# Reordering the products of a blocked down projection so that a norm can lie inside it

## The reference

```python
    gate, up = jnp.split(hn @ w_gate_up, 2, axis=-1)
    return h + (jax.nn.silu(gate) * up) @ w_down          # D_FF = 2816
...
    x = rms_norm(h, final_g)[:, N_META:]                  # end of the first block
...
    h = rms_norm_2(x, pre_norm_g[layer])                  # start of the second block
    proj = h @ w_in[layer]
    a_u, a_v, sq, sk, sv, mq, z = jnp.split(proj, split_at, axis=-1)
    mkv = rms_norm_2(mem, mem_norm_g[layer]) @ w_mem_kv[layer]     # 256 memory rows
```

## Time and profile before

| | |
|---|---|
| Time, 3 runs | 2336.96, 2339.67, 2341.39 us; median 2339.67 |
| The profiled execution | 2337.65 us, of it span 2335.9 us from first to last instruction |
| PE busy | 2195.0 us, 94% of the span |
| DVE, ACT, POOL busy | 1434.1, 907.7, 1013.5 us |
| Granted TensorE clock, mean | 0.976 of 2.4 GHz |
| Down projection on PE | from 1589.8 us to 1805.5 us of the span |
| First turn of x on PE | at 1872.86 us |

### The profile page before, as it was taken

The page is one execution under the profiler, slowest core; times in us unless marked ns, Lnnn a source line. Parts: engine busy times, 40 slices in busy tenths (PEclk is TensorE's granted clock), DMA queues, the critical chain, the costliest instruction groups (busy, mean ns, idle before and its releaser), DMA issues.

```text
span 2335.9 us, 29848 instructions
## 1 busy us (share of the span) xinstructions
PE 2195.0 (94%) x10756; PEld 1807.1 (77%) x10756; DVE 1434.1 (61%) x2790; ACT 907.7 (39%) x1626; POOL 1013.5 (43%) x584
## 2 busy tenths in 40 slices
PE   7999999999999989999989999999999798998896
PEld 6886688998887767778768888888887676878774
DVE  4258799999903567653886565655477607207713
ACT  5234522233225655433433233334445334126622
POOL 1265333465553232236665555555588413120042
PEclk9999999999999989999999999999999799999998
DMA  5112111111242221056244544457754121110212
GB/s 183 52 46 68 55 55 45 55 46 41 73 125 87 64 95 41 28 171 194 86 140 140 171 140 172 140 191 276 250 187 138 44 101 39 52 55 6 91 42 89
DMA packets 244837, 237.94 MB, mean 102 GB/s; under 512 B 10449, under 2 KB 186222, under 8 KB 244702
## 3 DMA queue, kind: packets, MB, share of 16 engines
q1 hardware_dynamic: 240544, 222.97, 29.3%
q10 hardware_dynamic: 4158, 13.16, 1.4%
HBM read 174.01 MB, written 61.15 MB: 101 GB/s over the span
## 4 chain that ended last, share of the span: by engine, by line
PE 71%; DVE 10%; ACT 3%; issue 3%; POOL 1%; DMA 0%; ACTq 0%; DVEq 0%; SPq 0%
PE ps L927 23%; PE ps L1214 16%; PE ps L1239 9%; PE ps L1283 8%; PE ps L1104 6%; PE ps L1438 4%; PE ps L1136 1%; DVE logit L2213 1%; PE ps L1079 1%; PE ps L1122 1%; ACT p_s L2035 1%; DVE pt_lo L2232 1%; PE ps L1361 0%; DVE logit L2226 0%; DVE yz L2757 0%
## 5 line engine op out<-in xcount | busy, mean ns | idle before, releaser
L2810 POOL TENSOR_TENSOR w_lo<-w_raw,w_hi 128x1024 fp32r<-128x1024 f32 (+1 forms) x143 | 312.5, 2186 | 877.3 <-ACT w_hi L1470 877.3
L927 PE MATMUL ps<-x_hi,w_hi 128*128 128x512 f32 (+2 forms) x960 | 361.6, 377 | 4.0 <-DVE c_rs L2130 3.3
L927 PE MATMUL ps<-x_lo,w_hi 128*128 128x512 f32 (+2 forms) x960 | 359.8, 375 | 0.0
L927 PE MATMUL ps<-x_hi,w_lo 128*128 128x512 f32 (+2 forms) x960 | 357.7, 373 | 0.0
L927 PEld LDWEIGHTS ps<-x_hi,w_hi 128*128 128x128 f32 x960 | 181.5, 189 | 39.7 <-issue 9.4
L927 PEld LDWEIGHTS ps<-x_hi,w_lo 128*128 128x128 f32 x960 | 181.8, 189 | 28.8
L927 PEld LDWEIGHTS ps<-x_lo,w_hi 128*128 128x128 f32 x960 | 181.3, 189 | 28.6 <-issue 0.2
L1470 ACT CAST w_hi<-w_raw 128x1024 fp32r<-128x1024 f32 (+1 forms) x143 | 135.4, 949 | 161.7 <-PE ps L927 73.0
L2188 DVE MATCH_REPLACE8 score<-best,score 128x400 f32<-128x400 f32 (+3 forms) x224 | 185.2, 830 | 0.0
L2184 DVE MAX8 best<-score 128x8 f32<-128x400 f32 (+3 forms) x224 | 181.3, 843 | 1.4
L1283 PE MATMUL ps<-x_hi,w_hi 128*128 128x512 f32 (+1 forms) x416 | 153.9, 370 | 3.6 <-POOL x_lo L2971 2.3
(11 more groups left out here) (441 smaller groups left out, 5286.0 us busy)
## 6 DMA issues: line engine op xcount, KB each, us to landing
w_raw<-in_w_in SPq DMA_DIRECT2D x74, 512.0 KB, 3.7
wdr<-as_scratch SPq DMA_DIRECT2D x77, 256.0 KB, 3.5
rawg<-in_w_gate_up SPq DMA_DIRECT2D x22, 512.0 KB, 3.9
rawu<-in_w_gate_up SPq DMA_DIRECT2D x22, 512.0 KB, 5.4
wdr<-in_w_down SPq DMA_DIRECT2D x22, 512.0 KB, 6.5
as_scratch<-ac SPq DMA_DIRECT2D x44, 256.0 KB, 3.8
wt_scratch<-wdr SPq DMA_DIRECT2D x33, 256.0 KB, 4.7
as_scratch<-a SPq DMA_DIRECT2D x33, 256.0 KB, 3.5
```

The lines of the kernel that those rows point to most:

```text
L927: mm = pe.matmul(ps[:, b, 0:n], w[:, s, P * k:P * k + P], r[:, k, t0:t0 + n], start=k == 0 and i == 0, stop=k == kd - 1 and i == 2 and ext ...
L2810: pool.tensor_tensor(w_lo[:, p % 2, 0:n], w_raw[:, p % 2, 0:n], w_hi[:, p % 2, 0:n], ALU.subtract).then_inc(wlo_done, 1)
```

## The change

The order of the seven products changes from the fifth on, so that the fourth and the fifth finish all eight pieces of token half 0, and the sixth and the seventh those of half 1. `down_sums` now adds the banks to d2 after the sixth product (p = 5) in place of the fifth. Squares and sums of pieces 4 to 7 lie in the first slots of the sixth product. In its slots j = 3 to 9 lie, for half 0: PE's column sums (behind step 58) and spread (behind step 60), the inverse, root and four diagonal blocks, and the eight chunks with their splits (slots 6 to 9, two each). The ring of combined activations moves to the other token half of x_hi and x_lo from step 54 on, d4 and accumulators get other places. The seventh product waits until the eight chunks have been made, since one of its banks holds the spread factor. After the last step only half 1 is left; the panels au 0 and au 1 run half 0 first, then half 1; and the spread of the second factor, which x waits for, comes behind these panels.

```diff
@@ plan, FINAL
-    for m in range(2):
-        panel(("au", m), 2)
+    panels += [("au", 0), ("au", 1)]
+    ticks += [(("au", m), j) for j in range(2) for m in range(2)]
...
-        FINAL = [(f, 0) for f in range(4)] + [(f + 4, 1) for f in range(4)] + [(f, 1) for f in range(4)] + [(f + 4, 0) for f in range(4)]
+        FINAL = [(m, 0) for m in range(8)] + [(f + 4, 1) for f in range(4)] + [(f, 1) for f in range(4)]
@@ SP
             def down_weights(p, j):
                 return (w_dn[P * j:P * j + P, 0:BANK], wt_scratch[1, j], wt_scratch[0, j], w_dn[P * (HJ + j):P * (HJ + j) + P, 0:BANK],
-                        wt_scratch[2, j], wt_scratch[3, j], w_dn[P * (HJ + j):P * (HJ + j) + P, BANK:D])[p]
+                        w_dn[P * (HJ + j):P * (HJ + j) + P, BANK:D], wt_scratch[2, j], wt_scratch[3, j])[p]
@@ PE, down_step
                     if j == 0 and p >= 3:
-                        pe.wait_ge(dn_done, (4 * (p - 3) + f + 1) if p < 6 else 12 + 2 * f + 2)
+                        pe.wait_ge(dn_done, 4 * (p - 3) + f + 1)
+                    if j == 0 and p == 6:
+                        pe.wait_ge(xn_done, XN_0 + KD)
@@ PE
+            def final_norm_sums(h, b):
+                pe.wait_ge(acc2a_done, 7 * (h + 1))
+                pe.wait_ge(acc2b_done, 7 * (h + 1))
+                for st in range(2):
+                    for i in range(4):
+                        mm = pe.matmul(ps[:, b, 4 * st + i:4 * st + i + 1], acc2[st][h][:, P * i:P * i + P], ones[:, 0:1], start=True, stop=True)
+                mm.then_inc(stat_full, 1)
+
+            def final_norm_spread(h, b):
+                pe.wait_ge(diag_done, 8 + 4 * h + 4)
+                pe.matmul(ps[:, b, :], ones[:, :], n_diag[:, HALF[h][0]:HALF[h][0] + BANK], start=True, stop=True).then_inc(rs_full, 1)
...
             for s in range(STEPS):
                 down_step(s)
+                if s == 5 * HJ + 3:
+                    final_norm_sums(0, 0)
+                if s == 5 * HJ + 5:
+                    final_norm_spread(0, 1)
                 if s == 6 * HJ + 4:
                     memory_turned()
...
+            for m in range(2):
+                pe.wait_ge(dn_done, 24 + m + 1)
+                linear(("mk", m), 0, memt_hi, memt_lo, 0, MEM)
             pe.wait_ge(dn_done, 28)
             for m in range(2):
                 linear(("mv", m), 0, memt_hi, memt_lo, 0, MEM)
+                if m == 0:
+                    final_norm_sums(1, 3)
+            linear(("au", 0), 0, x_hi, x_lo, 0, BANK)
+            final_norm_spread(1, 7)
+            linear(("au", 1), 0, x_hi, x_lo, 0, BANK)
             for m in range(2):
-                panel2(("au", m))
+                linear(("au", m), 1, x_hi, x_lo, BANK, BANK)
+            for h, (t0, w) in enumerate(HALF):
+                pe.wait_ge(diag_done, 16 + 4 * h + 4)
+                pe.matmul(ps[:, 4 + h, :], ones[:, :], n_diag2[:, t0:t0 + w], start=True, stop=True).then_inc(rs_full, 1)
 
             pe.wait_ge(x2_done, KD)
@@ ACT, in slot s
-                if p >= 4 and 2 <= j < 6:
+                if p in (4, 6) and 2 <= j < 6:
                     final_squares(4 * (p - 4) + j - 2)
+                if p == 5 and j < 2:
+                    final_squares(4 + 2 * j)
+                    final_squares(5 + 2 * j)
+                if s == 5 * HJ + 4:
+                    final_root(0)
+                if p == 5 and 6 <= j < 10:
+                    normed_high(2 * j - 12)
+                    normed_high(2 * j - 11)
@@ ACT, after the last step
+            final_squares(12), (13), memory_panel(0), final_squares(14), (15), memory_panel(1), (2), final_root(1), memory_panel(3), normed_high(8..15), u_tile(0,0), u_tile(1,0), ...
@@ DVE, in slot s
+                if p == 5 and 1 <= j < 3:
+                    final_sums(2 + 2 * j)
+                    final_sums(3 + 2 * j)
+                if s == 5 * HJ + 4:
+                    final_inverse(0, 0)
+                if s == 5 * HJ + 5:
+                    final_factor(0)
+                if p == 5 and 6 <= j < 10:
+                    normed_chunk(2 * j - 12, 1)
+                    normed_chunk(2 * j - 11, 1)
+                    normed_low(2 * j - 11)
@@ POOL, in slot s
-                if p >= 3 and j == 1:
+                if p >= 3 and j == (3 if p == 5 else 1):
                     with_residual(p)
+                if p == 5 and 1 <= j < 3:
+                    final_sums(2 + 2 * j)
+                    final_sums(3 + 2 * j)
+                if p == 5 and 6 <= j < 10:
+                    normed_low(2 * j - 12)
```

More of the change, by code:

```diff
@@ L365, in build, with sr @@
         a_cmb = [piece(f"ac{k}", k, 1) for k in range(4)]
-        sr_hi = [(x_hi[:, k, 0:BANK]) for k in range(SLOTS)]
-        sr_lo = [(x_lo[:, k, 0:BANK] if k < 4 else x_hi[:, k + 2, 0:BANK]) for k in range(SLOTS)]
+        def sr(low, s):
+            k = s % SLOTS
+            if s >= 5 * HJ - 1:
+                return (x_lo if low else x_hi)[:, k, BANK:S]
+            return x_hi[:, k, 0:BANK] if not low else x_lo[:, k, 0:BANK] if k < 4 else x_hi[:, k + 2, 0:BANK]
         d1 = place("d1", [P, 4, BANK], F32, W_RAW)
         d2 = place("d2", [P, 4, BANK], F32, W_RAW + BLOCK)
-        d4 = place("d4", [P, 4, BANK], F32, 1152 + 6 * BLOCK)
-        n_acc2 = place("n_acc2", [P, 2, S], F32, 1152 + 7 * BLOCK)
-        n_sq2 = [place("n_sqa", [P, 2, BANK], F32, ST), place("n_sqb", [P, 2, BANK], F32, ST + 8 * S)]
+        late = [place(f"late{f}", [P, BANK], F32, 1152 + f // 2 * KD * T * 4 + (6 + f % 2) * T * 4 + BANK * 4) for f in range(4)]
+        d4 = [late[f][:, :] for f in range(4)]
+        acc2 = [[place(f"acc2{st}", [P, BANK], F32, RA - 36 * S + 2 * S * st), late[st]] for st in range(2)]
+        n_sq2 = [place("n_sqa", [P, 2, BANK], F32, RA + 24 * S), place("n_sqb", [P, 2, BANK], F32, ST + 8 * S)]
         RS = 1152 + 2 * KD * T * 4 + 6 * KD * P * 4
@@ L1930, in _ @@
                     split(AT2[PANELS2[1]])
-            for z in range(12, 16):
-                final_squares(z)
-            norm()
+            final_squares(12)
+            final_squares(13)
+            memory_panel(0)
+            final_squares(14)
+            final_squares(15)
+            memory_panel(1)
+            memory_panel(2)
+            final_root(1)
+            memory_panel(3)
+            for q in range(KD, 2 * KD):
+                normed_high(q)
             def v_panel(m):
@@ L1941, in v_panel, with u_tile @@
                 behind2(("av", m))
+            def u_tile(m, j):
+                t0, w = HALF[j]
+                b = tile2(("au", m), j)
+                act.activation(yz[:, m, t0:t0 + w], ps[:, b, :], ACT.Gelu_apprx_tanh).then_inc(au_done, 1)
             def u_panel(m):
-                for j, (t0, w) in enumerate(HALF):
-                    b = tile2(("au", m), j)
-                    act.activation(yz[:, m, t0:t0 + w], ps[:, b, :], ACT.Gelu_apprx_tanh).then_inc(au_done, 1)
+                for j in range(2):
+                    u_tile(m, j)
                 behind2(("au", m))
+            u_tile(0, 0)
+            u_tile(1, 0)
             for m in range(2):
-                u_panel(m)
+                u_tile(m, 1)
+                behind2(("au", m))
             for n in range(16):
@@ L2294, in two, with diagonal @@
                 return ap.rearrange("p (n w) -> p n w", n=2)
-            def diagonal(which, out_):
-                for b in range(NB):
+            def diagonal(which, out_, blocks):
+                for b in blocks:
                     dve.tensor_scalar(out_[:, P * b:P * b + P], ident[:, :], nst[:, which, b:b + 1], None, ALU.mult).then_inc(diag_done, 1)
@@ L2592, in _ @@
+                if s == 5 * HJ + 5:
[4 more added lines that the diff above has]
+                    normed_low(2 * j - 11)
                 if s == 6 * HJ + 7:
                     memory_low()
-            for z in range(12, 16):
-                final_sums(z)
-            dve.wait_ge(stat_full, 3)
-            dve.tensor_scalar(nst[:, 0, :], ps[:, 4, 0:8], 1.0 / D, EPS, ALU.mult, ALU.add).then_inc(nst_step, 1)
@@ L2614, in _ @@
+            final_inverse(1, 3)
+            final_factor(1)
+            for q in range(KD, 2 * KD):
+                normed_chunk(q, 7)
+                if q % 2:
+                    normed_low(q)
+            diagonal(4, n_diag2, range(NB))
             for m in range(KD):
@@ L3094, in _ @@
                     split(AT2[PANELS2[1]])
-            for z in range(12, 16):
-                final_sums(z)
+            final_sums(12)
+            final_sums(13)
+            behind2(("mk", 0))
+            final_sums(14)
+            final_sums(15)
+            behind2(("mk", 1))
+            behind2(("mv", 0))
+            behind2(("mv", 1))
+            for q in range(KD, 2 * KD, 2):
+                normed_low(q)
             pool.wait_ge(c2_load, 7 * 16)
```

157 lines of the change are left out of this document (74 added, 83 removed).

## The result

| | before | after |
|---|---|---|
| Time, median of 4 runs each on one chip | 2340.53 us | 2356.24 us (2355.06 to 2358.6) |
| Ratio, 95% interval | | 1.007 (1.0053 to 1.0088) |
| The profiled execution: time, span | 2337.65, 2335.9 us | 2355.1, 2353.4 us |
| Granted TensorE clock, mean | 0.976 | 0.974 |

The kernel became 0.7% slower, 15.7 us by the medians and 17.5 by the two spans. The forecast was 2355.0 and 15.6 more. The busy times on the page hardly moved against the earlier trace rows, which is the first thing to see: no work was added. PE's busy time grew by 3.5 us and its idle time by 14.0, so the 17.5 us are PE's waits and the slow clock behind them.

A forecast was written before the change was run, and what follows sets the result against it. The prediction took the kernel to be bound by PE, busy 94% of the span. Added 29.3 us less 13.7 won in the tail gives 15.6 more: 2353.3 for the profiled execution, median near 2355, range 2340 to 2367.

The forecast's parts named there:

- The sums' wait: Sixth product, after step 58: PE waits 8.7 us for the sums of squares, bounds 5.5 and 10.
- The sums and the clock: Sixth product: column sums take 3.5 us at clock 0.50, and slow matmuls behind them lose 2.0.
- The spread: Sixth product, after step 60: PE waits 4.1 us, spread takes 1.3, slow matmuls behind lose 1.6.
- The wait at the seventh product: Before the seventh product: PE waits 6.5 us for the eighth chunk, at 4.9 per slot; clock loss 1.6.
- The tail: Last step to first turn of x: 53.7 us where it was 67.4, so 13.7 won.
- The spell of low clock: Tail: one slow spell in its short gaps adds 1.6 us.
- the 0.5 for cold turns: End of the tail: turns of x starting at low clock after 9.6 idle us add 0.5.
- Smaller waits: Rival: waits at lower bounds 5.5, 3.3, 1.6, clock loss as priced; 3 us more, 2343; chance 0.18.
- The clock stays down: Rival: no recovery between waits, steps 59 to 65 run slow; 13 us more, 2368; chance 0.09.
- Full exclusion: Rival: DVE and POOL take strict turns, each contended op costs 2.0 us; 2359; chance 0.05.
- The engines keep pace: Rival: DVE and POOL do not hinder each other, waits 2.4, 3.3, 1.6; 5.7 us less, 2334; chance 0.09.
- DVE's total (38.9 of 30.4 us): Sixth product: added work gives DVE 38.9 us in a 30.4 us window, so it cannot go at PE's pace.

The follow-up runs named there:

- experiment 3: Against the changed kernel, DVE instead of POOL also adds the second sums of squares of pieces 4 to 7; 2356.48 us, ratio 1.0078.
- experiment 4: Against experiment 3, POOL's four residual additions to mix moved from slot 58 to slot 60; 2358.62 us, ratio 1.0081.
- Experiment 2: Against the changed kernel, dummy fp32 matmuls fill PE's waits before the sums, the spread and the seventh product; 2352.0 us, ratio 1.0058.
- experiment 6: Against the changed kernel, experiment 1's tail, half 0's norm spread over two products, seventh product no longer waiting for the chunks; 2327.6 us, ratio 0.9951.
- experiment 5: Against the changed kernel, half 0's column sums and spread three steps later, all eight chunks in slot 64; 2351.91 us, ratio 1.006.
- experiment 7: Against experiment 6, the spread and eight chunks of half 0 moved behind the last step; 2327.75 us, ratio 0.995.
- experiment 1: Against the changed kernel, second factor's diagonal blocks before the half-1 chunks, its spreads directly behind the first spread; 2346.76 us, ratio 1.004.
- experiment 8: Against experiment 6, second factor's blocks back behind the half-1 chunks, its spreads behind the au panels; 2335.67 us, ratio 0.9987.

## Why the prediction was right, point by point

**The sums' wait** was forecast as 8.7 and is 8.3, ended by POOL's second pair of sums, as the text had it. Squares in pairs, two buffers, 1.7 per contended op: experiments 3 and 4 show that price where POOL is busy and 0.6 where it is not, on the same line.

**The sums and the clock.** 3.5 forecast, 3.54 measured, at 0.50. Twelve matmuls behind them came 0.43 apart: 2.4 us lost, 2.0 forecast. Experiment 2 shows the cause, since the same sums behind filled waits take 1.92.

**The spread.** Its wait is 3.7 (4.1 forecast), it took 1.87 (1.3), and only four matmuls were slow behind it (0.8 where 1.6 was forecast).

**The wait at the seventh product** is 6.7 (6.5 forecast), with slots of 4.9 us exactly as worked out, and nine slow matmuls behind it (1.8 where 1.6 was forecast). The sixth product thus takes 58.15 us up to the seventh's first matmul, 27.7 more than 30.4, where about 27 were forecast.

Together 8.3 + 3.5 + 2.4 + 3.7 + 1.9 + 0.8 + 6.7 + 1.8 = 29.1, against 29.3 forecast. From the last step's end before to its end after it is 30.3 (1805.5 to 1835.8), of which 0.35 lie ahead of the sixth product; 0.8 I cannot assign.

**The tail** was mis-sized, not misunderstood: 56.3 for 53.7. The spell of low clock came at its size: the matmuls of mv 1 started 0.21 apart, not 0.12, from 1849.77 to 1853.4, which is the 1.6 of the forecast. The term that was short is the chunks. The eight of half 1 took 12.9 (from 1860.93 to 1873.82, 3.24 for each pair) and not the 9.8 read from the earlier trace rows. That reading was wrong: the stretch from 1850.38 to 1860.20 holds seven chunks, not eight, and DVE waits 1.2 us in it, while here each pair waits 0.7 for ACT's high part, 2.8 in all. So au waited 2.6 for x_lo where the forecast had no such wait. Another 0.4 is that mv 1 began late. Against these, the 0.4 for a bank that ACT frees did not come, and the 0.5 for cold turns lies behind the first turn. About half a microsecond stays unassigned.

**Behind the first turn** nothing was forecast, and 1.8 us were won: 461.25 for 463.04. The traces place the gain within the first 20 us. The four turns of w_sp start 12.0 after the first turn, not 12.7, the first panel behind them 13.9 after it, not 15.1, and its first matmuls run at a granted clock of 1.00, where in the kernel before they ran at 0.61. That makes 2.2 us, of which 0.4 are lost again further on. Why PE waited less for ACT among the turns stays open.

30.3 - 11.0 - 1.8 = 17.5 us, the difference of the spans (15.6 forecast), while the medians lie 15.7 apart. That the median fell within 1.2 of the forecast owes something to chance: the tail's miss (+2.6) and what came off behind it (-1.8) are of opposite sign, and the spans alone would put the miss at 1.9.

**The rivals.** "Smaller waits" fell with the waits at their forecast size. "The clock stays down" fell: in the windows it comes back each time. Full exclusion fell by the rows: 1.7 per pair of ops and 4.9 per slot, not 2.0. (By the Trainium skill, "SBUF — State Buffer", section "Who interferes with whom", the two engines exclude each other for a whole instruction; the trace agrees that they get into each other's way. By the same section of the Trainium skill, a DVE op with at most one input in SBUF, outside the 2-port modes, is not in GpSimd's way; the trace agrees for the four additions of banks to mix, which from 1743.14 take 2.48, 0.6 each, beside POOL's low parts. But the sum by it is 0.3 per op too high, or 0.2 if one adds up starts, 0.60 + 1.26; so it fell as a price, and that the two engines take turns for a part of each op is not excluded. And the last section has ops of another kind, with one input in SBUF, that POOL did slow; in which mode they ran no trace shows.) "The engines keep pace" was, in the kernel as changed, false; experiment 6 shows that it is true of another placement of the same work. That the change itself could have been laid out so was not seen in the prediction, which asked only what this layout does.

**What I would not have said so again.** The prediction had it that work put into the sixth product is won or lost by DVE's total (38.9 of 30.4 us). Experiments 5, 6 and 7 say more: the total says that a wait will come, and the barrier (the seventh product's first wait) says where. In experiment 6 the chunks lie in the next product, and in experiment 7 in the tail, at no measurable cost. How much of this is the barrier, and how much that the load was spread over more slots, is argued and not shown, since both kernels change both.

## What to carry to other kernels

Before work is moved beside a busy engine, count what its neighbours already do there, and look for the barrier that makes an overrun count. Here three waits each looked curable, and shortening one (experiments 4 and 5) lengthened another by about as much or more. They went only when the barrier was moved and the work spread out. Where work is taken off the end, ask what lay beside it: here a 9.6 us scaling lost its cover, and putting its factor first gave back 7 to 9 us (experiments 1 and 8), more than the 3 to 5 that all the rest of the new layout brought at its best. A wait on TensorE has a second price, the matmuls behind it at half clock, here up to a third of the waits' length (6.3 of 18.7, counted from the mark in one execution; by the medians and ratios 2 to 3, not clear of noise).

## What the runs showed of the hardware that I had not expected

A DVE op with one SBUF input and a per-partition scalar (a diagonal block, 128x128 fp32) takes 0.2 us alone, and 0.97 (3.88/4) beside POOL's additions; I had charged such ops nothing for company. Even ops on 128x4 grew: the factor product, with two inputs in SBUF, from 0.15 to 1.21, and one row in the tail of the kernel after took 1.95 (here with POOL's low part beside it):

```profile
1850.12 1.95 DVE L2604 TENSOR_SCALAR nst<-nst 128x4 f32<-128x4 f32 x1
```

It was 0.17 in the kernel before, with POOL idle. Three times this row ended 0.02 to 0.04 us behind POOL's instruction: at 1774.09 and at 1852.07 in the kernel after, and at 1830.57 in experiment 6. Not every small op is held: beside the first of these POOL instructions the reciprocal took 0.18, and the ops with an input in PSUM 0.15 and 0.16. An op that is held can take about as long as one of POOL's (1.3 to 2.4 here), and a chain of such ops pays that several times. And twenty fp32 matmuls that compute nothing, put into waits of 18.7 us, shortened the way to the seventh product by 4.1 us: the granted clock stayed at 1.00 through the first wait, where it had fallen to 0.50.
